# Mixture-of-experts stage: quarter rows gathered, 32x32 blocks turned by VectorE, weighted expert rows added in DRAM

## The reference, cut to what matters

```python
logits = h @ w_router + b_router            # h = rmsnorm(x), 512 x 1024; 32 experts
top_v, top_i = top_k(logits, 4);  top_w = softmax(top_v)
for each expert e, on the rows (tokens) sent to it:
    gu   = rows @ w_gate_up[e] + b_gate_up[e]          # 1024 -> 2048
    gate = minimum(gu[:, :1024], 7); up = clip(gu[:, 1024:], -7, 7)
    act  = (up + 1) * gate * sigmoid(1.702 * gate)
    y[token] += top_w * (act @ w_down[e] + b_down[e])  # 1024 -> 1024
x = x + y;  x = rmsnorm(x, norm_final)
```

## Time and profile before

| | |
|---|---|
| median of 3 runs | 2275.82 us (2270.96 to 2276.48) |
| the profiled execution | 2271.97 us |
| its span | 2270.1 us |
| TensorE busy (matmuls) | 2149.2 us, 95% of the span |
| VectorE, ScalarE, GpSimd busy | 723.0, 510.4, 233.1 us |
| mean granted TensorE clock | 0.975 |
| DMA over the whole span | 525.69 MB, mean 232 GB/s |

### The profile page before, as it was taken

One profiled execution on the slowest core, in us unless ns is written; L12 is line 12 of the kernel. 1 busy time (PEld: TensorE's weight loads), 2 busy tenths in 40 slices (PEclk: granted clock), 3 DMA queues, 4 the chain that ended last, 5 costly groups with the idle time before them and its releaser, 6 DMA issues.

```text
span 2270.1 us, 42773 instructions
## 1 busy us (share of the span) xinstructions
PE 2149.2 (95%) x18148; PEld 1309.6 (58%) x18148; DVE 723.0 (32%) x1235; ACT 510.4 (22%) x758; POOL 233.1 (10%) x323
## 2 busy tenths in 40 slices
PE   6999898599999999999999999979998988999998
PEld 5879766234434434434434444436776677888887
DVE  4444433311111111111111111125465433445444
ACT  4242332001101101100100100123345733222221
POOL 1010000001011011011011111112200210000000
PEclk9999999799999999999999999989999999999999
DMA  7324112789999999999999999955211011323221
GB/s 245 98 93 152 61 38 111 312 341 393 389 386 388 392 386 383 395 375 397 387 387 389 388 393 389 389 202 186 75 57 56 1 44 50 111 92 95 90 94 54
DMA packets 148529, 525.69 MB, mean 232 GB/s; under 512 B 12236, under 2 KB 59392, under 8 KB 115616
## 3 DMA queue, kind: packets, MB, share of 16 engines
q1 hardware_dynamic: 137968, 500.20, 58.1%
q0 software_dynamic: 10512, 24.79, 3.4%
HBM read 516.93 MB, written 16.79 MB: 235 GB/s over the span
## 4 chain that ended last, share of the span: by engine, by line
PE 75%; DVE 3%; ACT 2%; POOL 1%; DMA 1%; issue 1%; ACTq 0%; DVEq 0%; POOLq 0%
PE ps L1957 29%; PE ps L1971 15%; PE ps L390 7%; PE ps L392 7%; PE ps L391 7%; PE ps L1929 1%; PE ps L1856 1%; PE ps L1949 1%; PE ps L1937 1%; POOL rstd L464 1%; PE ps L1848 1%; PE ps L1866 1%; PE ps L1766 1%; PE ps L1924 1%; PE ps L485 1%
## 5 line engine op out<-in xcount | busy, mean ns | idle before, releaser
L1957 PE MATMUL ps<-ring_a,xe 128*32 128x512 f32 x3912 | 434.9, 596 | 0.0
L1971 PE MATMUL ps<-ring_a,act_t 128*32 128x256 f32 x6000 | 336.1, 380 | 1.5 <-ACT ye L1070 1.5
L1957 PEld LDWEIGHTS ps<-ring_a,xe 128*32 128x32 f32 x3912 | 127.7, 111 | 281.7 <-issue 276.0
L1971 PEld LDWEIGHTS ps<-ring_a,act_t 128*32 128x32 f32 x6000 | 191.9, 110 | 143.4 <-issue 25.6
L1957 PE MATMUL ps<-ring_b,xe 128*32 128x512 f32 x2232 | 251.6, 594 | 0.0
L390 PE MATMUL ps<-xt_hi,hi 128*128 128x512 f32 x576 | 229.4, 398 | 5.6 <-DVE xt_lo L498 4.7
L392 PE MATMUL ps<-xt_hi,lo 128*128 128x512 f32 x576 | 227.2, 395 | 0.0
L391 PE MATMUL ps<-xt_lo,hi 128*128 128x512 f32 x576 | 226.8, 394 | 0.0
L1058 ACT ACTIVATE glu<-ps 128x768 f32<-128x768 f32 x32 | 25.9, 810 | 656.0 <-PE ps L1957 656.0
L1957 PEld LDWEIGHTS ps<-ring_b,xe 128*32 128x32 f32 x2232 | 69.6, 110 | 151.1 <-issue 148.2
L390 PE MATMUL ps<-hi,xt_hi 128*128 128x512 f32 (+1 forms) x384 | 147.6, 384 | 7.4 <-DVE lo L377 5.2
(11 more groups left out here) (302 smaller groups left out, 2496.7 us busy)
## 6 DMA issues: line engine op xcount, KB each, us to landing
ring_a<-in_w_gate_up SPq DMA_DIRECT2D x163, 1024.0 KB, 8.0
ring_a<-in_w_down SPq DMA_DIRECT2D x125, 1024.0 KB, 7.8
ring_b<-in_w_gate_up SPq DMA_DIRECT2D x93, 1024.0 KB, 7.0
raw<-in_w_in SPq DMA_DIRECT2D x20, 1024.0 KB, 7.5
raw<-in_w_gate SPq DMA_DIRECT2D x11, 1024.0 KB, 5.3
raw<-in_w_up SPq DMA_DIRECT2D x11, 1024.0 KB, 5.3
raw<-in_w_down SPq DMA_DIRECT2D x11, 1024.0 KB, 4.8
raw<-in_w_out SPq DMA_DIRECT2D x8, 1024.0 KB, 5.1
```

The lines of the kernel that those rows point to most:

```text
L1957: last = pe.matmul(ps[QUAD * j:QUAD * j + QUAD, g, :], xe[:, k, QUAD * g:QUAD * g + QUAD], w[:, j, :, :], start=False, stop=k == KT - 1)
L1971: last = pe.matmul(y_block(g, j), act_t[:, 2 * g + h, QUAD * c:QUAD * c + QUAD], w[:, h, QF * j:QF * j + QF], start=c == 0 and h == 0 and ...
```

## The change

Nothing is changed in the weights' ring, in the number of blocks or in the matmuls of L1957 and L1971, but for the order in which the 32-column groups of weights and rows are paired.

- `norm_rows` writes the rows of the mixture's norm with their columns permuted (four instructions of 256 columns each in place of one of 1024), and `w_router` is permuted to match.
- `gather` is three indirect DMAs of 128 quarter rows (1 KB each) in place of one of 96 rows of 4 KB. Partition 32j+c gets quarter j of slot c, so that `x_transpose`, one VectorE instruction that turns 32x32 blocks in place, gives `xe`. `act_transpose` does the same for `act_t`. All 14 TensorE transposes and the copies `x_evacuate` and `act_evacuate` go.
- x is stored to `x_rows` in DRAM ahead of the loop, with 96 spare rows in front. `scatter` adds `ye` to `x_rows` (`compute_op=ALU.add`) where it wrote to `y_rows`; empty slots now name the spare rows, so that all 384 quarter rows are moved.
- `y_evacuate` multiplies by the routing weight (three ScalarE instructions in place of two); the weights of a block come from a second selection (`sel_w`, `wx`) and a slot sum of 192 columns in place of 96.
- After the loop SyncE reads x back (four loads of 512 KB); `combine` is one addition of the down bias from PSUM. The diagonals, their matmuls and the four products per tile go. The bias matmuls of all tiles stand ahead of it, in banks of their own.

```diff
@@ norm_rows @@
+            if NS["ffn"] <= s < NS["ffn"] + T:
+                h = h.rearrange("p (j b c) -> p j b c", j=4, b=KT)
...
+                for j in range(4):
+                    i = dve.scalar_tensor_tensor(h[:, j, :, :], src[:, j, :, :], rstd[:, s:s + 1], w[:, j, :, :], ALU.mult, ALU.mult)
@@ sync_program @@
+            for t in range(T):
+                evacuated(sp, SA, SA.first[A_END - 1] + t)
+                sp.dma_start(x_tile_rows(t), x[:, t, :]).then_inc(x_set, 16)
+            sp.dma_start(x_dram[0:4 * CAP, :].rearrange("(s j) c -> s (j c)", j=4), x[0:CAP, 0, :]).then_inc(x_set, 16)
...
-                sp.dma_start(yk(t), y_dram.rearrange("(k s j) c -> s k (j c)", k=TOPK, j=4)[t * P:(t + 1) * P, :, :])\
-                  .then_inc(row_tile[t], 16)
+                sp.dma_start(x[:, t, :], x_tile_rows(t)).then_inc(row_tile[t], 16)
@@ gather, scatter @@
-            pool.indirect_dma_start(xg[:, :], None, h_dram, bass.IndirectOffsetOnAxis(ap=idx_g[:, :].bitcast(U32), axis=0),
+            for g in range(GROUPS):
+                pool.indirect_dma_start(xg[:, g, :], None, h_dram, bass.IndirectOffsetOnAxis(ap=idx_g[:, g:g + 1].bitcast(U32), axis=0),
...
-                pool.indirect_dma_start(y_dram, bass.IndirectOffsetOnAxis(ap=idx[:, g:g + 1].bitcast(U32), axis=0),
+                pool.indirect_dma_start(x_dram, bass.IndirectOffsetOnAxis(ap=idx[:, g:g + 1].bitcast(U32), axis=0),
...
+                                        compute_op=ALU.add).then_inc(m_scat, 16)
@@ moe_scalar @@
+            def y_evacuate(scattered, weighted, w):
                 act.wait_ge(m_scat, scattered)
-                act.activation(ye[:, 0:2, :].rearrange("p g c -> p (g c)"), ps[:, 3, :], ACT.Copy)
-                act.activation(ye[:, 2, :], ps[:, 4, 0:QF], ACT.Copy).then_inc(m_y, 1)
+                act.wait_ge(m_idx, weighted)
+                for g in range(GROUPS):
+                    i = act.activation(ye[:, g, :], ps[:, 3 + g // 2, QF * (g % 2):QF * (g % 2) + QF], ACT.Copy,
+                                       scale=w[:, g:g + 1])
@@ moe_vector @@
+            def act_transpose(n, used):
+                dve.wait_ge(m_act, n + 1)
                 dve.wait_ge(m_used, used)
+                dve.transpose(flat(act_t), flat(act_e)).then_inc(m_at, 1)
+
+            def x_transpose(n, used):
+                dve.wait_ge(m_gathered, n * 48 + 48)
...
+                dve.transpose(flat(xe), flat(xg)).then_inc(m_x, 1)
@@ moe_tensor, the loop @@
                     if j == 2:
-                        pe.wait_ge(m_y, i + 1)
                         slot_sums(i + 2)
-                pe.wait_ge(m_at_a, i + 1)
-                pe.wait_ge(m_at_v, i + 1)
-                pe.wait_ge(m_idx, i + 3)
-                for c in range(3):
+                pe.wait_ge(m_at, i + 1)
+                pe.wait_ge(m_y, i + 1)
+                for c in range(4):
                     down_chunk(c, 16 + c, i * 16 + 32)
-                x_transposes(i + 2)
-                pe.wait_ge(m_act, i + 2)
-                act_transposes(i + 1)
-                down_chunk(3, 19, i * 16 + 32)
```

More of the change, by code:

```diff
@@ L47 @@
 C_QUAD = C_OWN + CAP
-C_EYE = C_QUAD + 1
+C_PAD = C_QUAD + 1
+C_EYE = C_PAD + GROUPS
 C_ALL = C_EYE + MAXB + 1
@@ L886, in scalar_program @@
             moe_scalar(act)
-            for t in range(T):
-                for k in range(TOPK // 2):
-                    i = act.activation(diag[:, t, k, :], ident, ACT.Copy, scale=top_w[:, t, k:k + 1])
-            i.then_inc(diag_set, 1)
             hi_part(act, SB, 0)
@@ L1474, in route @@
             link(dve.tensor_tensor(dst[:, :, :], mask[:, :, :], b3(cc(C_TOK, T), NE), ALU.mult))
-            for k in range(1, TOPK):
-                link(dve.scalar_tensor_tensor(dst[:, :, :], oh(k), float(k * SEQ), dst[:, :, :], ALU.mult, ALU.add))
             dve.wait_ge(r_pos, 1)
@@ L1508, in route_weights @@
                 link(i) if k < TOPK - 1 else i.then_inc(r_mask, 1)
+            dve.wait_ge(r_mask, 3)
+            for q in range(PASSES):
+                dve.tensor_copy(wx[:, :, NE * q:NE * q + NE], w_full[:, :, :])
+            link(dve.memset(wx[:, :, MAXB:MAXB + 1], 0.0))
         def moe_vector(dve, link_route):
@@ L1518, in link, with select @@
                 dve.wait_ge(moe_dve_step, base_[0] + steps[0])
-            def select(n):
+            def select(n, before):
                 dve.wait_ge(m_pos, n)
@@ L1525, in select, with indices @@
                                           ALU.is_equal, ALU.mult)
+                if before is not None:
+                    for t in range(T):
+                        i = dve.tensor_scalar(sel_w[:, t, :], cc(C_SLOT, CAP), posx[:, t, bass.ds(before, 1)],
+                                              wx[:, t, bass.ds(before, 1)], ALU.is_equal, ALU.mult)
                 link(i)
-                dve.reduce_sum(own[:, :], sel[:, :, :].rearrange("p t s -> p s t"), AX.X).then_inc(m_sel, 1)
-            def indices(n, scattered, gathered):
+                i = dve.reduce_sum(own[:, 0, :], sel[:, :, :].rearrange("p t s -> p s t"), AX.X)
+                if before is not None:
+                    i = dve.reduce_sum(own[:, 1, :], sel_w[:, :, :].rearrange("p t s -> p s t"), AX.X)
+                i.then_inc(m_sel, 1)
+            def indices(n, scattered, gathered, parts=2):
                 dve.wait_ge(m_pos, n + 1)
@@ L1919, in moe_tensor, with slot_sums, columns @@
             n1 = pe.value_load(n_blk[0:1, 0:1], min_val=NE - 1, max_val=MAXB - 1)
[L1921 removed]
+            def slot_sums(n, parts=2):
                 pe.wait_ge(m_sel, n + 1)
[L1924 to L1940 removed]
+                pe.matmul(ps[:, 6, 0:parts * CAP], cc(C_ONES), own[:, 0:parts, :], start=True, stop=True)\
+                  .then_inc(m_pos, 1)
+            def columns(w):
+                return w.rearrange("p (u b j c) -> p j u b c", u=2, b=KT, j=4)
             def gate_up_open(n):
```

211 lines of the change are left out of this document (90 added, 121 removed).

## The result

| | before | changed |
|---|---|---|
| median | 2275.51 us | **2220.4 us** (2218.99 to 2221.1, 4 runs) |
| ratio | | 0.9761, 95% interval 0.9746 to 0.9775 |
| span of the profiled execution | 2270.1 us | 2218.5 us |
| last down matmul ends | 1515.4 | 1474.4 |
| first matmul of the next block | 1559.0 | 1507.4 |

The kernel is 55 us faster. The forecast was 24 (2252 us); 2220 is what the first rival gave (2219). The change in the span, 51.6 us, splits into 41.0 in the loop and 10.6 after it. The first expert matmul starts at 426.28 where it started at 426.52, and from the next block's first matmul to the end it is 711.1 us in both: the head and the rest count for nothing.

What follows compares the result with a forecast made beforehand. The prediction took TensorE to pace the old loop with the DMA stream close behind, and the stream to bound the new one: -7.9 in the loop and -16 after it gave -24, 2252 us at the median (range 2219 to 2268).

Steps and rivals of the forecast that it cites:

- the first rival: Expert loop: the DMA stream keeps up and TensorE sets the pace; -57 us, 2219 at the median; chance 0.20.
- the head: Before the loop: five stores, added gather issues and the first turn cost +1 us (0 to +4).
- the stream's need: Expert loop: DMA time a block for weights, gather and scatter becomes 34.5 us (33.2 to 36.6).
- the old stream's need: Loop before the change: 33.2 us a block, the 33.75 us pass with 0.5 of slack taken.
- gather in quarter rows: Loop's gather: moves the same bytes in quarter rows, so its cost stays at 1.7 us a block.
- scatter: more rows, and adding: Loop's scatter: 384 rows for about 256, each added in DRAM, counted by bytes read: 1.25 us more a block.
- the DMA share: Old loop: DMA engines busy for the whole pass, share 1.00, held against the stream having slack.
- The sum of the count: Loop end along SyncE's queue: 432.9 + 31 x 34.5 + 5.2 = 1507.6, 7.9 us less than 1515.5.
- TensorE's part: Down stage: transposes go (1.53 us), slot sum grows 0.17; net 1.36 us a block, pass 32.4 us.
- The signs: Loop: 32.4 us periods, then near 34.5, landings growing to about 30 us, would show the forecast right.
- the mechanism of the forecast: Expert loop goes from TensorE's pace to the slower DMA stream's, so much of the matmuls' gain is not collected.
- The tail: After the loop: accumulate's landing +2, read of x -3.4, chain to next matmuls -14.8; sum -16 us (-20 to -10).

Runs made afterwards that it cites:

- c_spread: Changed kernel, half the down matmuls left out, plain scatter, one gather of 64 rows of 4 KB spread over 96 partitions: stream needs 32.2 us a block.
- f_turns: Changed kernel with 14 TensorE transposes of a constant put back in the down stage, read by nothing: 2262.6 us, ratio to before 0.9945.
- f_rows: Changed kernel with empty slots' indices out of bounds again, so only rows with a token are added; spare rows go: median 2212.4 us.
- f_plain: Whole changed kernel with the scatter writing in place of adding: 2213.2 us (one run).
- f_base: The changed kernel itself run again, as the mark for further versions on the same chip: median 2216.9 us.
- f_tail: Changed kernel, after the loop only: oh_b and rel_w loads and matmuls moved earlier, last block's ye in its own buffer: median 2215.7 us.
- f_extra: Whole changed kernel with one more plain scatter of 384 quarter rows a block, into a table nobody reads: 2257.7 us (one run).
- c_after: Changed kernel with half of the down stage's matmuls left out, gather and adding scatter kept: stream needs 33.1 us a block.

## Why the prediction was wrong, step by step

**The step that failed** is the stream's need: "The need becomes 34.5 us (33.2 to 36.6), over the 32.4 of TensorE." Measured it is 33.1, just under the lower end of its bounds. By terms:

| term | forecast | measured |
|---|---|---|
| the old stream's need | 33.2 (slack 0.5 of 33.75) | 32.66 (slack 1.1) |
| gather in quarter rows | no change | **-0.95** |
| scatter: more rows, and adding | +1.25 | +0.29 + 1.10 = +1.39 |
| new need | 34.5 | 33.1 |

The need came out 1.4 too high: 0.95 by the gather, 0.5 by the slack, less 0.14 for the scatter. The adding, the one operation that no row showed, was sized well. What failed was the term "The new gather moves the same bytes in quarter rows, as the old scatter did; I leave it at 1.7": the old gather cost 1.85, by c_spread mostly for where its rows lay, the new one 0.9. And the slack was taken from how late loads landed (7.8 us, 2.7 over a lone one), which does not give it: in f_turns they land after 7.3 us with 0.8 us of slack, in the kernel before after 7.8 with 1.1. Nor does the DMA share, which I held against rival 1: it was 1.01 with 1.1 us of slack.

**The sum of the count was off by a second term,** that worked the other way: 31 passes from 432.9 on. The first takes 40 us, not one of the stream's, so the count misses about 7 us. With the true need and this, the last load of the changed kernel would land at 432 + 40 + 29.9 x 33.1 + 7 = 1469, and it does at 1467.8. At my need of 34.5 the same count ends some 6 us later than mine. (A reading was off too, without effect: the plateau of the earlier trace rows has seventeen slices, not eighteen.)

**TensorE's part was right.** Forecast -1.36 us a pass, 32.4; f_rows and f_plain show 32.27, that is -1.48, and the transposes put back cost 1.61. The slot sum took 0.14 more at its place, of the 0.17 that I gave. "-42 + 1" was the loop's sum for the first rival, and -41.0 was measured; that they agree is in part luck. The full gain is -45, as in f_rows. Of the 4 us between them 0.7 lie in the last two passes of the profiled execution, where the ring's lead ends, and 3.4 in the slower passes of its first third, whose cause is open; what else differs is small and cancels.

**The signs.** Rival 1 was to show a constant period with landings under 15 us. The period came, the landings did not: they went the forecast's way, up to 28 us. The mechanism of the forecast is at work in the changed kernel, and by f_base against f_rows it costs 3.7 us there in place of 34. No matmul of L1957 got longer (596 ns before and after).

**The tail gave 10.6 of 16.** The chain after the loop shows where (start, us, what):

```profile
1468.34 7.59 DMA x_rows<-ye,idx_s
1476.03 1.21 ACT ye L1076 x3
...
1479.95 2.83 POOL x_rows L758
...
1485.02 2.99 DMA rel_w<-in_rel_bias
1488.06 1.86 PE ps L1780 x2
...
1491.18 3.79 PE ps L1784 x4
...
1507.42 0.47 PE ps L390
```

ScalarE waits 1.6 us for the scatter of the block before (the old one had landed by then); the last three issues take 6.9 us where 3.6 stood, and the landing 1.0 more: 6.1 in all, where I gave 2. The read of x is 3.8 us shorter (3.4 forecast), and from its landing to the next block's first matmul it is 16.6 us where it was 29.5, so 12.9 of my 14.8. That rest is TensorE, which waits for `rel_w` (issued behind the last scatter) and so keeps the second tile's addition until 1495.06; in f_tail's profile the wait is gone and the stretch is 3.2 us shorter, which its runs do not confirm.

**The head** was +1 by forecast, and 0.

## What to carry to other kernels

Where two limits lie close, measure the hidden one by taking work from the engine that hides it: one run with half of a stage left out gave the stream's need to 0.1 us, which no row of the kernel before could. In the changed kernel, where the stream had become the slower one, landing to landing gives it as well. A ring's lead is a store of time: a stream slower than its consumer is free until loads land as late as the ring is deep (here 28 us, with eleven of twelve chunks, 29.6 us, ahead), and from there every added microsecond is paid; so look at how issue-to-landing grows over the loop, not at its median. Many DMA rows that are out of bounds should not lie together in the partitions of one transfer: here it cost 0.66 us a block.

## What the runs showed of the hardware that I had not expected

- Quarter rows of 1 KB travel four to a packet of 4096 bytes (0.166 us), but rows that are added in DRAM travel one to a packet (0.101 us for 1024 bytes).
- GpSimd issues an adding indirect DMA of 128 rows in 1.59 us and a plain one in 1.02, in the same kernel and at the same place. The groups of GpSimd's instructions in f_extra, 530 to 1480 us:

```profile
L761 POOL DMA_INDIRECT x_rows<-ye,idx_s x85 | 135.3, 1591 | 33.0 <-issue 33.0
L765 POOL DMA_INDIRECT rows_twice<-ye,idx_fix x87 | 88.4, 1016 | 26.5 <-issue 26.5
```

- When loads land 20 us and more after their issue, a single DMA issue on SyncE's queue can take up to 12 us (11.6 us at 1397.73 in c_after), where 0.34 is usual: the issue itself waits. So the queue's period shows the stream's pace before TensorE loses anything, in f_base from 1053 us on, where TensorE's passes lengthen at 1272.
- A single gather of 64 rows of 4 KB costs the weight stream 1.85 or 1.2 us, by the partitions that they go to.
- Skipped rows are not free: 128 of 384 added rows set out of bounds (f_rows) saved the stream 0.4 us of a price of 1.97 for all.
